# Head norms of a two-layer mixer kernel: mean squares per token in 8 columns, with a TensorE turn back, and one projection unit in another bank

## The reference

```
def rms_norm(x, gain):
    xf = x.astype(jnp.float32)
    y = xf * lax.rsqrt(jnp.mean(xf * xf, axis=-1, keepdims=True) + EPS)
    return (y * gain.astype(jnp.float32)).astype(x.dtype)

fx, gqx, gkx, gvx, nqx, nkx, nvx, gatex = jnp.split(ux @ w_in, PROJ_SPLITS, axis=-1)
gk_h = rms_norm(heads(gkh, GQA_KV_HEADS), k_norm)                       # context keys
q = apply_rope(rms_norm(heads(gqx, GQA_HEADS), q_norm), cos, sin)       # 8 query heads
k = apply_rope(rms_norm(heads(gkx, GQA_KV_HEADS), k_norm), cos, sin)    # 2 key heads
y_f = fourier_mix(fx) @ w_fourier                                       # 2-D DFT, group by group
yx = gated_merge(gatex, y_f, y_g, y_n) @ w_o
```

## Time and profile before

| | us |
|---|---|
| median of 3 runs (2015.85 to 2019.09) | 2018.73 |
| the profiled execution, own time | 2018.0 |
| its span | 2016.2 |
| TensorE busy in it | 1958.6 (97%) |
| VectorE / ScalarE / GpSimd busy | 816.2 / 655.5 / 1004.9 |
| mean granted TensorE clock | 0.996 of full |

### The profile page before, as it was taken

How to read it: one execution, slowest core, us unless ns; L and a number is a source line. 1 busy time by engine, 2 the same in 40 slices (tenths; PEclk the granted TensorE clock), 3 DMA queues, 4 the chain that set the end, 5 groups by cost and what they waited for, 6 DMA issues and landing times.

```text
span 2016.2 us, 28399 instructions
## 1 busy us (share of the span) xinstructions
PE 1958.6 (97%) x10081; PEld 1584.2 (79%) x10081; DVE 816.2 (40%) x1331; ACT 655.5 (33%) x1031; POOL 1004.9 (50%) x835
## 2 busy tenths in 40 slices
PE   6999999999999999999999999999999799999998
PEld 4777777787667888878877887788788677997887
DVE  4222122357762224623122354221223775466454
ACT  4211211243452223412211243122123444444433
POOL 2444444343213544444544445454445433987997
PEclk9999999999999999999999999999999999999999
DMA  9555655443112333453344236524523521655664
GB/s 340 171 182 179 195 187 181 122 112 109 43 43 63 100 98 103 154 185 121 116 158 135 75 112 211 173 86 146 175 78 92 154 74 53 182 172 154 186 185 133
DMA packets 413576, 279.26 MB, mean 139 GB/s; under 512 B 25346, under 2 KB 398588, under 8 KB 406060
## 3 DMA queue, kind: packets, MB, share of 16 engines
q1 hardware_dynamic: 401868, 206.79, 34.7%
q10 hardware_dynamic: 11520, 71.05, 9.6%
q0 software_dynamic: 96, 0.16, 0.0%
HBM read 276.92 MB, written 1.05 MB: 138 GB/s over the span
## 4 chain that ended last, share of the span: by engine, by line
PE 89%; DVE 5%; issue 2%; SPq 1%; ACT 1%; POOL 1%; DMA 1%; DVEq 0%; POOLq 0%; ACTq 0%
PE bank L1346 25%; PE bank L1347 25%; PE bank L1348 25%; PE bank L1355 4%; PE bank L1464 3%; PE bank L1354 2%; PE bank L1706 1%; PE bank L1659 1%; PE bank L1724 1%; POOL w_lo L520 1%; SPq L425 1%; DMA mod_first<-in_mod_w 1%; DVE tmp L962 1%; DVE u_lo L975 1%; PE bank L1353 1%
## 5 line engine op out<-in xcount | busy, mean ns | idle before, releaser
L520 POOL TENSOR_TENSOR w_lo<-w_raw,w_hi 128x512 fp32r<-128x512 f32 (+2 forms) x824 | 1002.3, 1245 | 1000.2 <-ACT w_hi L552 999.5
L1346 PE MATMUL bank<-u_hi,w_hi 128*128 128x512 f32 (+1 forms) x1704 | 636.2, 373 | 9.6 <-DVE u_lo L975 9.0
L1348 PE MATMUL bank<-u_hi,w_lo 128*128 128x512 f32 (+1 forms) x1704 | 627.2, 368 | 0.0
L1347 PE MATMUL bank<-u_lo,w_hi 128*128 128x512 f32 (+1 forms) x1672 | 618.9, 370 | 0.0
L552 ACT ACTIVATE w_hi<-w_raw 128x1024 fp32r<-128x1024 f32 (+2 forms) x412 | 385.9, 968 | 182.4 <-PE bank L1348 159.2
L1346 PEld LDWEIGHTS bank<-u_hi,w_hi 128*128 128x128 f32 x1704 | 322.4, 189 | 88.7 <-DVE hf L1051 21.0
L1348 PEld LDWEIGHTS bank<-u_hi,w_lo 128*128 128x128 f32 x1704 | 322.2, 189 | 53.8
L1347 PEld LDWEIGHTS bank<-u_lo,w_hi 128*128 128x128 f32 x1672 | 316.4, 189 | 51.8 <-issue 0.5
L1051 DVE TENSOR_TENSOR hf<-bank,sg 128x512 f32<-128x512 f32 (+1 forms) x85 | 53.2, 626 | 537.9 <-ACT sg L658 535.6
L658 ACT ACTIVATE sg<-bank 128x512 f32<-128x512 f32 (+1 forms) x85 | 46.3, 545 | 637.7 <-PE bank L1348 573.6
L1346 PE MATMUL bank<-h_hi,w_hi 128*128 128x512 f32 (+1 forms) x539 | 209.5, 389 | 0.0
(11 more groups left out here) (193 smaller groups left out, 1988.2 us busy)
## 6 DMA issues: line engine op xcount, KB each, us to landing
w_raw<-in_ffn_w_in SPq DMA_DIRECT2D x176, 512.0 KB, 3.8
mod_w<-in_mod_w ACTq DMA_DIRECT2D x56, 1024.0 KB, 6.9
w_raw<-in_w_in SPq DMA_DIRECT2D x68, 512.0 KB, 3.7
w_raw<-in_ffn_w_out SPq DMA_DIRECT2D x64, 384.0 KB, 3.4
w_raw<-in_ffn_w_out SPq DMA_DIRECT2D x64, 320.0 KB, 3.3
mod_first<-in_mod_w SPq DMA_DIRECT2D x4, 2048.0 KB, 14.4
mod_w<-in_mod_w ACTq DMA_DIRECT2D x16, 512.0 KB, 5.8
w_raw<-in_w_o SPq DMA_DIRECT2D x16, 512.0 KB, 4.4
```

The source lines that it names most:

```text
L520: pool.tensor_tensor(w_lo[:, slot, k0:k1, :], w_raw[:, slot, k0:k1, :], w_hi[:, slot, k0:k1, :].bitcast(F32), ALU.subtract).then_inc(S("w_ ...
L1346: pe.matmul(dst, w_hi[:, slot, kk, :], hi_, start=start, stop=False)
L1347: pe.matmul(dst, w_hi[:, slot, kk, :], lo_, start=False, stop=False)
L1348: return pe.matmul(dst, w_lo[:, slot, kk, :], hi_, start=False, stop=stop)
```

## The change

Each head's mean square is now computed with the squares as the stationary operand, 128 tokens at a time, and 2 columns of `head_mean` (one for each head) as the moving one. The result is 2 columns for each 128 tokens: 8 columns for 512 tokens, 4 for 256, with the token in the partition. Root and reciprocal run over these columns. A copy then lays each reciprocal out 64 times beside itself in `rstd`, and TensorE turns the layout back with a 128x128 transpose for each 128 tokens, into bank 4, from which `head_norm` reads it. DVE's part before the transpose is the new `head_rows`, TensorE's is `spread_roots`.

Unit 4 goes to bank 5, where the spread `rstd` of the whole token was before, and follows the second pair directly; units 5, 6 and 7 go to banks 0, 1 and 2. TensorE's order becomes unit 4, statistics(0), unit 5, spread_roots(0), channels(0), statistics(1), unit 6, spread_roots(1), swap(0), channels(1), statistics(2), unit 7, spread_roots(2), swap(1), positions(0), statistics(3), positions(1), spread_roots(3), swap(2), statistics(4), swap(3), scores(0), spread_roots(4), turn_v. The statistics now wait for the norm before them, since its reciprocals lie in bank 4, and `swap` waits for the copy of unit 4 out of bank 5.

```
+    HEAD_BANK = [0, 1, 2, 3, 5, 0, 1, 2]
...
-                act.activation(root[:, 0:n], bank[:, 4, 0:n], ACT.Sqrt, bias=eps_col[:, 0:1]).then_inc(S("qk_root"), 1)
+                act.activation(root[:, 0:2 * n // P], bank[:, 4, 0:2 * n // P], ACT.Sqrt, bias=eps_col[:, 0:1]).then_inc(S("qk_root"), 1)
...
+            def head_rows(c):
+                n = head_tokens(l, HEAD[QK[c]][0])
+                cols = 2 * n // P
+                dve.wait_ge(S("qk_root"), 5 * l + c + 1)
+                link(dve.reciprocal(rstd_col[:, 0:cols], root[:, 0:cols]))
+                dve.tensor_copy(rstd[:, 0:n].rearrange("p (a d) -> p a d", d=HD), rstd_col[:, 0:cols].unsqueeze(2).to_broadcast([P, cols, HD]))\
+                   .then_inc(S("qk_rows"), 1)
+
             def head_norm(c):
...
-                link(dve.reciprocal(rstd[:, 0:n], root[:, 0:n]))
-                dve.scalar_tensor_tensor(out=qk[:, c, 0:n], in0=qk[:, c, 0:n], scalar=gain, in1=rstd[:, 0:n],
+                dve.wait_ge(S("qk_spread"), 5 * l + c + 1)
+                dve.scalar_tensor_tensor(out=qk[:, c, 0:n], in0=qk[:, c, 0:n], scalar=gain, in1=bank[:, 4, 0:n],
                                          op0=ALU.mult, op1=ALU.mult).then_inc(S("qk_normed"), 1)
...
-                wait(pe, S("qk_root"), 5 * l + c)
-                pe.matmul(bank[:, 4, 0:n], head_mean[:], head_sq(c, n), start=True, stop=True).then_inc(S("qk_ms"), 1)
+                wait(pe, S("qk_normed"), 5 * l + c)
+                means = head_mean[:].rearrange("p (h d) -> p h d", d=HD)[:, :, 0]
+                for a in range(n // P):
+                    last = pe.matmul(bank[:, 4, 2 * a:2 * a + 2], head_sq(c, n)[:, P * a:P * a + P], means, start=True, stop=True)
+                last.then_inc(S("qk_ms"), 1)
+
+            def spread_roots(c):
+                n = head_tokens(l, HEAD[QK[c]][0])
+                pe.wait_ge(S("qk_rows"), 5 * l + c + 1)
+                for a in range(n // P):
+                    last = pe.transpose(bank[:, 4, P * a:P * a + P], rstd[:, P * a:P * a + P], ident[:])
+                last.then_inc(S("qk_spread"), 1)
...
             def swap(c):
                 pe.wait_ge(S("qk_normed"), 5 * l + c + 1)
+                pe.wait_ge(S("qk_raw"), 5 * l + 3)
...
+            pe.wait_ge(S("rstd_copied"), k)
+            unit(4, HEAD_BANK[4])
             statistics(0)
             pe.wait_ge(S("qk_raw"), 5 * l + 1)
-            unit(4, 0)
+            unit(5, HEAD_BANK[5])
+            spread_roots(0)
             channels(0)
...
```

More of the change, by code:

```diff
@@ L223, in build @@
     rsum = sb("rsum", [P, 2, 2])
-    rstd_col = sb("rstd_col", [P, 2 * TT])
+    rstd_col = sb("rstd_col", [P, 2 * TOK // P])
     row_sq = sb("row_sq", [P, 2 * TT])
@@ L775, in _ @@
             hi_ahead(10)
-            copy_head(7, vT[:, 0, :], 3).then_inc(S("head_copied"), 1)
+            copy_head(7, vT[:, 0, :], HEAD_BANK[7]).then_inc(S("head_copied"), 1)
             hi_ahead(11)
@@ L1161, in raw @@
                 else:
-                    dve.tensor_copy(qk[:, c, 0:n], bank[:, idx % 4, 0:n]).then_inc(S("qk_raw"), 1)
+                    dve.tensor_copy(qk[:, c, 0:n], bank[:, HEAD_BANK[idx], 0:n]).then_inc(S("qk_raw"), 1)
+            def head_rows(c):
[5 more added lines that the diff above has]
+                   .then_inc(S("qk_rows"), 1)
             def head_norm(c):
@@ L1166, in head_norm @@
                 gain = vec[:, l, V_KN:V_KN + 1] if c == 0 else gq[:, l:l + 1]
-                dve.wait_ge(S("qk_root"), 5 * l + c + 1)
-                link(dve.reciprocal(rstd[:, 0:n], root[:, 0:n]))
-                dve.scalar_tensor_tensor(out=qk[:, c, 0:n], in0=qk[:, c, 0:n], scalar=gain, in1=rstd[:, 0:n],
+                dve.wait_ge(S("qk_spread"), 5 * l + c + 1)
+                dve.scalar_tensor_tensor(out=qk[:, c, 0:n], in0=qk[:, c, 0:n], scalar=gain, in1=bank[:, 4, 0:n],
                                          op0=ALU.mult, op1=ALU.mult).then_inc(S("qk_normed"), 1)
@@ L1220, in _ @@
             raw(1)
+            head_rows(0)
+            raw(2)
             head_norm(0)
-            raw(2)
             spectrum(0)
+            head_rows(1)
+            raw(3)
             head_norm(1)
             rope(0)
-            raw(3)
             spectrum(1)
+            head_rows(2)
+            raw(4)
             head_norm(2)
             rope(1)
-            raw(4)
             fourier(0)
+            head_rows(3)
             head_norm(3)
@@ L1234, in _ @@
             fourier(1)
+            head_rows(4)
             rope(3)
@@ L1613, in _ @@
                 pair(ph, [(idx, 0), (idx + 1, 0)], [idx, idx + 1], [n, n1], k, idx == 0)
+            pe.wait_ge(S("rstd_copied"), k)
+            unit(4, HEAD_BANK[4])
             statistics(0)
             pe.wait_ge(S("qk_raw"), 5 * l + 1)
-            unit(4, 0)
+            unit(5, HEAD_BANK[5])
+            spread_roots(0)
             channels(0)
             statistics(1)
+            pe.wait_ge(S("qk_raw"), 5 * l + 2)
+            unit(6, HEAD_BANK[6])
+            spread_roots(1)
             swap(0)
-            pe.wait_ge(S("qk_raw"), 5 * l + 2)
-            unit(5, 1)
             channels(1)
             statistics(2)
+            pe.wait_ge(S("head_copied"), 3 * l + 1)
+            unit(7, HEAD_BANK[7])
+            spread_roots(2)
             swap(1)
-            pe.wait_ge(S("head_copied"), 3 * l + 1)
-            unit(6, 2)
             positions(0)
             statistics(3)
+            positions(1)
+            spread_roots(3)
             swap(2)
-            pe.wait_ge(S("head_copied"), 3 * l + 2)
-            unit(7, 3)
-            positions(1)
+            statistics(4)
             swap(3)
@@ L1734, in _ @@
                 if p == 0:
-                    statistics(4)
+                    spread_roots(4)
                     pe.wait_ge(S("cat_ready"), DC * l + 1)
```

## The result

The changed kernel takes 2022.78 us (median of 20 runs, 2019.68 to 2025.66), and the kernel before 2019.42 (20 runs, 2015.85 to 2024.03). The ratio is 1.0017, with a 95% interval of 1.0011 to 1.0023: slower by about 3.4 us. The forecast was 2.5 us less than before, 2016.2 us, and its range ended at 2020.0. The direction, the time and the range all missed.

The account below looks back on a forecast made before the run. TensorE, busy 97%, was taken as the bound, so others matter only where it waits. Layer 0 +1.0 us and layer 1 -3.5 gave -2.5: 2018.73 to 2016.2 us, 0.12% faster, range 2013.0 to 2020.0.

Parts of the forecast that it names:

- Removed waits: Waits of statistics(0) and swap(0) go: -2.31 us in layer 0, net -6.71 in layer 1 including the clock.
- Statistics and spreads: On TensorE, statistics add 0.2 and 0.1 us; new transposes, 0.43 us for four, add 2.15 and 1.3.
- The new tail: From swap(2) to scores(0), waits of statistics(4) and swap(3) add 1.0 us in layer 0, 1.8 in layer 1.
- The clock: Layer 1, behind swap(0)'s wait: the low clock at 1606 to 1608 goes, saving 1.63 us.
- Rival 3: Layer 1's shorter waits still bring the clock down once, returning 1.63 us: -0.9 us in all, 2017.8; chance 0.08.
- rival 2: GpSimd holds up VectorE in both tails, norm(3) to last rows, adding 3.7 us: +1.2 in all, 2019.9; chance 0.10.
- Rival 4: Layer 1's statistics(1) waits for norm(0) behind spread_roots(0), 0.5 us at most, inside the range; no chance of its own.
- Nothing behind the scores changes: After the scores in both layers, attention steps pace each other and swap(4) keeps unit 8 ahead: no change in time.

Follow-up runs that it names:

- Experiment 4: The changed kernel with ScalarE's high weights of units 10 and 11 moved behind root_head(4), so GpSimd starts their low weights later; 2017.81 us, ratio 0.9995.
- experiment 2: The changed kernel's columns, rows and spreads, with units in the order and banks of the kernel before; 2021.49 us, ratio 1.0010 to the kernel before.
- experiment 1: The changed kernel's order and banks, with the wide statistics and reciprocals of the kernel before and no spreads; 2020.88 us, ratio 1.0011.

## Why the prediction was wrong

- **Removed waits: right.** All four are gone. Unit 4 waits 0.98 us for GpSimd's low weights, as printed, 1.08 forecast with the pace.
- **Statistics and spreads: right.** The product behind the statistics starts 0.81 us after them (461.58, 462.39) and takes 0.1 more than the others to the next, 0.9 in all, and four transposes take 0.43. Statistics(1) in layer 1 came 0.24 us late: from channels(0) to it are 1.10 us, and 0.86 before. The sum had no term for it.
- **The new tail: wrong, by 2.2 us, and it is the step that decided.** The prediction put swap(3) at T + 2.35 in layer 0 and T + 2.55 in layer 1. T is where swap(2) starts, 494.55 and 1620.62. Swap(3) started at 497.88 and 1624.38: T + 3.33 and T + 3.76. The step that failed is the duration of rotation 2 on VectorE. Layer 0's was priced at 1.34, three clean instructions, and took 2.3 (495.42 to 497.7); layer 1's was 1.94 and took 2.9. I had the bound in hand, 1.42 for one instruction, and gave GpSimd's hold-up to layer 1 only and once. Experiment 4 shows it: with GpSimd elsewhere, swap(3) started at T + 2.34 in layer 0, my own figure, and at T + 2.20 in layer 1.
- **The clock: wrong by 1.63 us.** The forecast took the low clock as bound to layer 1's second long wait and credited it as removed. It fell once in the heads in every profile of the changed kernel. Rival 3 said this and got 0.08; its argument against, that the clock was full behind the single wait of 2.97 us, rested on one execution, and the second and third profile of before show the fall just there.
- **Rivals.** What came is the mechanism of rival 2, at 2.2 of its 3.7 us, and rival 3 together. Forecast -2.5, plus 2.2 of tail, plus 1.6 of clock, plus 0.2 of statistics(1): +1.5, which is what the heads show (136.4 against 135.0). I had given them 0.10 and 0.08 as cases that exclude each other, though nothing keeps them apart. Rival 4's wait of statistics(1) for a norm is at most these 0.24 us.
- **"Nothing behind the scores changes": not borne out.** The low clock at 1698 stands behind a wait of 2.0 us that both kernels have. It was met in two of three profiles after and one of three before: too few to call it caused by the change. Over all runs the clock accounts for 1.3 us more than before, give or take 0.6. The rest of the measured 3.4 us is not in the prediction's terms.
- **Open:** 0.7 us of the difference outside the heads and the clock, and what decides which wait the clock falls behind. No run was made for either.

## What to carry to other kernels

Before work is taken off an engine that TensorE waits for, ask whether the order can hide it. Here eight of the ten wide reciprocals cost TensorE no wait once a unit lay over each, and the last of each layer a wait of 1.8 and 1.0 us, while the columns that replaced them add about 3.4 us of transposes to TensorE. When units move to the front of an order, the pieces they used to separate meet at its end; write down what stands between each two dependent pieces there. Price every VectorE instruction whose inputs all lie in SBUF at its worst wherever GpSimd's work can fall on it and TensorE waits for it, and count a low clock as gone only if several profiles of one kernel have it at the same place.

## What the runs showed of the hardware

- A VectorE multiplication or addition of 256 columns with both inputs in SBUF takes 0.42 us, and 1.05 to 1.41 beside GpSimd's subtraction of two SBUF tiles. A copy of 256 columns inside SBUF took 1.19 in place of 0.29. Two-input instructions with one input in PSUM took the same with GpSimd at work or not: 0.42 and 0.48.
- The granted clock fell to 0.50 behind waits of TensorE as short as 1.11 us (experiment 2, layer 0) and 1.21 us, stayed 1.00 behind 2.35 us in the same execution as the latter and behind 3.11 us in experiment 1. A fall cost 1.5 to 1.6 us; experiments 1 and 2 each have one in layer 1's head that is twice as long.
- The same program, profiled three times, had its waits at nearly the same length and its low clocks at other places. One fall more or less moves a single execution by 1.5 us, as much as the whole structural difference of the two heads.
